# State-space stage: squares of x on 128 partitions, another place for the conditioning blocks and the tables of phases

## The reference, cut to what matters

```python
sh1, sc1, gt1, sh2, sc2, gt2 = adaln(c, w_mod[layer], b_mod[layer])       # c @ w_mod + b_mod, split in six
csh1, csc1, cgt1, csh2, csc2, cgt2 = adaln(c_ctx, w_mod[layer], b_mod[layer])
h_lat = modulate(rmsnorm(x_lat, norm_mix_pre[layer]), sh1[:, None], sc1[:, None])
h_ctx = modulate(rmsnorm(x_ctx, norm_mix_pre[layer]), csh1, csc1)
y_ctx, y_lat = s5_mixer(h_ctx, h_lat, s5_a_re[j], s5_a_im[j], ...)         # 128 groups of 16 columns, 64 complex states
```

## Time and profile before

| what | value |
|---|---|
| runs | 3567.32 us, the median of 3 (3565.69 to 3569.23) |
| profiled execution | 3563.7 us, 3.6 us under that median |
| its span, first to last instruction | 3561.5 us |
| granted clock of TensorE, mean | 0.954 of full speed |
| busy over the span | PE 92%, DVE 60%, ACT 39%, GpSimd 13% |
| chain that ended last, by engine | PE 82%, DVE 6%, GpSimd 5%, DMA 2% |

### The profile page before, as it was taken

One profiled execution on the slowest core, in us unless ns is written; L12 is line 12 of the kernel. 1 busy time (PEld: TensorE's weight loads), 2 busy tenths in 40 slices (PEclk: granted clock), 3 DMA queues, 4 the chain that ended last, 5 costly groups with the idle time before them and its releaser, 6 DMA issues.

```text
span 3561.5 us, 51912 instructions
## 1 busy us (share of the span) xinstructions
PE 3290.0 (92%) x21097; PEld 2763.7 (78%) x21097; DVE 2148.8 (60%) x1852; ACT 1386.6 (39%) x1390; POOL 480.1 (13%) x352
## 2 busy tenths in 40 slices
PE   5787889799999999886789999999989899999998
PEld 3445578688888888675678888888868788888887
DVE  7667755555555555699565555555654555555555
ACT  4446534433333333322234434433323344344332
POOL 2869900000000000096000000000000000000000
PEclk7789899899999999998799999999999999999999
DMA  9988865355555555344045555555524455555552
GB/s 304 299 279 255 262 219 188 94 188 182 185 189 188 188 188 188 107 141 148 33 156 168 186 189 188 185 190 184 184 92 141 140 183 186 188 188 188 189 183 89
DMA packets 351007, 643.12 MB, mean 181 GB/s; under 512 B 21599, under 2 KB 50359, under 8 KB 350519
## 3 DMA queue, kind: packets, MB, share of 16 engines
q1 hardware_dynamic: 309952, 561.68, 47.9%
q10 hardware_dynamic: 40951, 79.98, 6.6%
HBM read 637.54 MB, written 4.06 MB: 180 GB/s over the span
## 4 chain that ended last, share of the span: by engine, by line
PE 82%; DVE 6%; POOL 5%; issue 2%; DMA 2%; ACT 1%; DVEq 1%; SPq 0%; ACTq 0%; POOLq 0%
PE acc L436 49%; PE acc L437 25%; POOL cpow L1800 3%; DMA raw<-in_w_mod_dram 2%; POOL ptmp L1800 1%; DVE z L912 1%; DVE w_lo L758 1%; PE acc L1232 1%; PE acc L1249 1%; PE acc L516 1%; PE acc L528 1%; PE acc L459 1%; PE acc L1157 1%; PE acc L1216 1%; DVE hf L797 0%
## 5 line engine op out<-in xcount | busy, mean ns | idle before, releaser
L436 PE MATMUL acc<-xin,w_hi 128*128 128x512 f32 x5376 | 1914.6, 399 | 58.7 <-DVE xin L772 33.7
L758 DVE TENSOR_TENSOR w_lo<-raw,w_hi 128x2048 fp32r<-128x2048 f32 x488 | 1120.0, 2301 | 1082.0 <-ACT w_hi L612 1081.6
L437 PE MATMUL acc<-xin,w_lo 128*128 128x256 f32 x5376 | 1519.2, 283 | 0.0
L612 ACT ACTIVATE w_hi<-raw 128x2048 fp32r<-128x2048 f32 x488 | 934.2, 1917 | 1367.7 <-PE acc L437 1366.7
L436 PEld LDWEIGHTS acc<-xin,w_hi 128*128 128x128 f32 x5376 | 1016.8, 189 | 312.7 <-issue 36.5
L437 PEld LDWEIGHTS acc<-xin,w_lo 128*128 128x128 f32 x5376 | 1021.0, 190 | 0.0
L436 PE MATMUL acc<-hid,w_hi 128*128 128x512 f32 x2432 | 845.4, 392 | 0.0
L437 PE MATMUL acc<-hid,w_lo 128*128 128x256 f32 x2432 | 681.2, 280 | 0.0
L436 PEld LDWEIGHTS acc<-hid,w_hi 128*128 128x128 f32 x2432 | 455.1, 187 | 101.3
L437 PEld LDWEIGHTS acc<-hid,w_lo 128*128 128x128 f32 x2432 | 459.6, 189 | 0.0
L764 DVE TENSOR_REDUCE tmp<-acc 128x1024 f32<-128x2048 f32 x116 | 264.9, 2284 | 19.9 <-PE acc L437 19.9
(11 more groups left out here) (239 smaller groups left out, 2057.8 us busy)
## 6 DMA issues: line engine op xcount, KB each, us to landing
raw<-in_ffn_w_gate_dram SPq DMA_DIRECT2D x88, 1024.0 KB, 5.0
raw<-in_ffn_w_up_dram SPq DMA_DIRECT2D x88, 1024.0 KB, 5.0
raw<-in_ffn_w_down_dram SPq DMA_DIRECT2D x88, 1024.0 KB, 5.0
raw<-in_w_mod_dram ACTq DMA_DIRECT2D x76, 1024.0 KB, 9.0
raw<-in_w_mlp_in_dram SPq DMA_DIRECT2D x64, 1024.0 KB, 5.4
raw<-in_w_mlp_out_dram SPq DMA_DIRECT2D x64, 1024.0 KB, 5.0
raw<-in_s_w_glu_dram SPq DMA_DIRECT2D x32, 1024.0 KB, 5.4
raw<-in_ab_w_in_dram SPq DMA_DIRECT2D x32, 1024.0 KB, 5.3
```

What stands on the lines that cost most here:

```text
L436: pe.matmul(bank, w_hi[:, slot, w], operand[:, kt, :], start=(kt == 0), stop=False)
L437: ins = pe.matmul(bank[:, 0:TOK], w_lo[:, slot, w], operand[:, kt, 0:TOK], start=False, stop=(kt == UK * units - 1))
L612: act.activation(w_hi[:, slot, :], raw[:, slot, :, :].rearrange("p k n -> p (k n)"), ACT.Copy).then_inc(hi_ready, 1)
L758: dve.tensor_tensor(w_lo[:, slot, :], raw[:, slot, :, :].rearrange("p k n -> p (k n)"), w_hi[:, slot, :].bitcast(F32), SUB).then_inc(lo_re ...
```

## The change

- `xs` has 128 partitions. A partition holds four tokens of 2048 columns: partitions 0 to 63 take ctx, 64 to 127 take x. There are two transfers, of 64 partitions and 2 MB each, and both are issued ahead of block 0. Four squares of 128 partitions take the place of eight of 64. The sums (`ss_x`, 128 by 4) are turned into 64 by 8 by two small matmuls with `sel_g`, which PE does ahead of `ada_rows(0)`, behind waits for the squares and for `angle_ready`.
- On DVE the scaling of the sums comes ahead of `powers_of_b(0)`, and the reciprocal ahead of `powers` of `ab` 2 and 3. ACT takes the root ahead of `copy_adarow(0, 1)`.
- Blocks 0 and 1 alone are consumed ahead of the rounds. The other 22 are placed by `BLOCKS_OF`: one block in rounds 0, 1, 2, 4, 6, 8, 10, 12, 14 and 15, two in rounds 3, 5, 7, 9, 11 and 13. The MOD blocks are spread over rounds 0 to 5. The SP queue loads block 2 after x of tile 1; all later blocks are on ACT's queue as before.
- `mod_columns(1)` to `(3)` move from after the first `ada_rows` of rounds 0, 3 and 5 to between `states` and `outputs` of rounds 2, 4 and 6, and PE waits for `mod_raw` after `outputs`.

```diff
-        xs = Region(xin_at, xin_at + 32 * KB)("xs", [64, L // 2, D])
+        xs = Region(xin_at, xin_at + 32 * KB)("xs", [P, L // 2, D])
...
+        xwide = [v.rearrange("(c f j) d -> (c f) j d", f=2, j=L // 2) for v in (ctx2, x2)]
...
-        MOD = [(0, 1), (2, 3), (6, 8), (10, 12)]
-        ADA = [4, 5, 7, 9, 11] + list(range(13, 24))
...
+        BLOCKS_OF = [[("mod", 1, 0)], [("mod", 1, 1)], [("mod", 2, 0)], [("mod", 2, 1), ("ada", 0)], [("mod", 3, 0)],
+                     [("mod", 3, 1), ("ada", 1)], [("ada", 2)], [("ada", 3), ("ada", 4)], [("ada", 5)], [("ada", 6), ("ada", 7)],
+                     [("ada", 8)], [("ada", 9), ("ada", 10)], [("ada", 11)], [("ada", 12), ("ada", 13)], [("ada", 14)], [("ada", 15)]]
+        FIRST_BLOCK = [2 + sum(len(v) for v in BLOCKS_OF[:r]) for r in range(KT + 1)]
...
-                    sp.dma_start(xs[s * NCH:(s + 1) * NCH, :, :], xch[s][:, 4 * half:4 * half + 4, :]).then_inc(xs_in, 16)
+                    sp.dma_start(xs[s * 64:(s + 1) * 64, :, :], xwide[s]).then_inc(xs_in, 16)
...
-            load_xs(0)
+            load_xs()
             ada_units(sp, 0)
             load_c(0)
             load_x(0)
-            sp.wait_ge(xs_sq, 4)
-            load_xs(1)
             ada_units(sp, 1)
-            ada_units(sp, 2)
             sp.wait_ge(c_sel, 1)
             load_c(1)
-            ada_units(sp, 3)
             sp.wait_ge(xt_scaled, 1)
             load_x(1)
+            ada_units(sp, 2)
             sp.wait_ge(c_sel, 2)
             load_c(2)
-            ada_units(sp, 4)
...
-            mod_rows(0, 0)
-            mod_rows(0, 1)
+            pe.wait_ge(xs_sq, 4)
+            pe.wait_ge(angle_ready, 1)
+            for f in range(2):
+                ins = pe.matmul(ps[2][0:64, 4 * f:4 * f + 4], sel_g[:, f * 64:(f + 1) * 64], ss_x[:, :], start=True, stop=True)
+            ins.then_inc(ss_tr, 1)
+            ada_rows(0)
+            ada_rows(1)
...
-            mod_rows(1, 0)
...
-            mod_rows(1, 1)
...
+                    m, n_blocks = FIRST_BLOCK[k + 1], len(BLOCKS_OF[k + 1])
+                if k in (1, 3, 5):
+                    mod_columns((k + 1) // 2)
                 if k >= 0:
                     outputs(k, k % 2)
+                if k in (1, 3, 5):
+                    pe.wait_ge(mod_raw, (k + 3) // 2)
                 if k + 1 < KT:
...
-                if 0 <= k < 4:
-                    mod_rows(2 + k // 2, k % 2)
+                if k + 1 < KT and n_blocks == 2:
+                    ada_rows(m + 1)
...
-                if 0 <= k < 4:
-                    ada_units(act, ADA[k + 1] + 2)
...
+                if k + 1 < KT and len(BLOCKS_OF[k + 1]) == 2:
+                    ada_units(act, FIRST_BLOCK[k + 1] + 2)
...
+            dve.wait_ge(ss_tr, 1)
+            dve.tensor_scalar(rstd_x[:, :], ps[2][0:64, 0:L], 1.0 / D, EPS, MUL, ADD).then_inc(ss_ready, 1)
             powers_of_b(c0, 0)
-            dve.wait_ge(xs_sq, 8)
-            dve.tensor_scalar(rstd_x[:, :], rstd_x[:, :], 1.0 / D, EPS, MUL, ADD).then_inc(ss_ready, 1)
-            powers([ab[:, 2], ab[:, 3]], uu, L)
             dve.wait_ge(rstd_root, 1)
             dve.reciprocal(rstd_x[:, :], rstd_x[:, :]).then_inc(rstd_ready, 1)
+            powers([ab[:, 2], ab[:, 3]], uu, L)
             modulation(cm, 0)
```

More of the change, by code:

```diff
@@ L107, in two_layer_kernel @@
         rstd_x = whole("rstd_x", [64, L])
+        ss_x = whole("ss_x", [P, L // 2])
         work_at = whole.at
@@ L1060, in _, with load_xs @@
                 sp.dma_start(braw[:, ri, :, :], b_view[ri]).then_inc(b_in, 16)
-            def load_xs(half):
+            def load_xs():
                 for s in range(2):
-                    sp.dma_start(xs[s * NCH:(s + 1) * NCH, :, :], xch[s][:, 4 * half:4 * half + 4, :]).then_inc(xs_in, 16)
+                    sp.dma_start(xs[s * 64:(s + 1) * 64, :, :], xwide[s]).then_inc(xs_in, 16)
             def load_c(n):
@@ L1150, in select_c, with ada_rows @@
                 ins.then_inc(c_sel, 1)
-            def ada_rows(m, window, units=range(UK)):
+            def ada_rows(m, units=range(UK)):
+                window = BLOCK_WINDOW[m]
                 for kk in units:
@@ L1159, in ada_rows @@
                     ins.then_inc(ada_unit, 1)
-            def mod_rows(b, v):
-                ada_rows(MOD[b][v], 47 - (16 + 4 * b + 2 * v))
             def mod_columns(b):
@@ L1289, in _ @@
                     states(k + 1, (k + 1) % 2)
+                    m, n_blocks = FIRST_BLOCK[k + 1], len(BLOCKS_OF[k + 1])
+                if k in (1, 3, 5):
+                    mod_columns((k + 1) // 2)
                 if k >= 0:
                     outputs(k, k % 2)
+                if k in (1, 3, 5):
+                    pe.wait_ge(mod_raw, (k + 3) // 2)
                 if k + 1 < KT:
-                    if k in (-1, 2, 4):
-                        pe.wait_ge(ada_sb, {-1: 2, 2: 3, 4: 4}[k])
-                    ada_rows(ADA[k + 1], 15 - (k + 1), (0, 1))
-                if k in (-1, 2, 4):
-                    mod_columns({-1: 1, 2: 2, 4: 3}[k])
+                    ada_rows(m, (0, 1))
                 if k + 2 < KT:
@@ L1308, in _ @@
                 if k + 1 < KT:
-                    ada_rows(ADA[k + 1], 15 - (k + 1), (2, 3))
+                    ada_rows(m, (2, 3))
                 if k + 2 < KT:
                     transpose_e(k + 2, 1)
-                if 0 <= k < 4:
-                    mod_rows(2 + k // 2, k % 2)
+                if k + 1 < KT and n_blocks == 2:
+                    ada_rows(m + 1)
                 if k == KT - 2:
@@ L1356, in copy_adarow, with square_x @@
                 act.activation(adarow[:, :], ps[0][:, :], ACT.Copy).then_inc(ada_sb, 1)
-            def square_x(half):
-                act.wait_ge(xs_in, 32 * (half + 1))
-                for j in range(4):
-                    act.activation(xs[:, j, :], xs[:, j, :], ACT.Square, accum_out=rstd_x[:, 4 * half + j:4 * half + j + 1]).then_inc(xs_sq, 1)
+            def square_x():
+                act.wait_ge(xs_in, 32)
+                for j in range(L // 2):
+                    act.activation(xs[:, j, :], xs[:, j, :], ACT.Square, accum_out=ss_x[:, j:j + 1]).then_inc(xs_sq, 1)
             def block_diagonal_b(n):
@@ L1433, in _ @@
             copy_b(1)
-            square_x(0)
+            square_x()
             copy_b(2)
@@ L1444, in _ @@
             copy_lam_powers(0)
-            square_x(1)
-            copy_adarow(0, MOD[0][1])
+            act.wait_ge(ss_ready, 1)
+            act.activation(rstd_x[:, :], rstd_x[:, :], ACT.Sqrt).then_inc(rstd_root, 1)
+            copy_adarow(0, 1)
+            act.wait_ge(c_sel, 1)
             copy_modulation(0)
             copy_c(0, 0)
-            act.wait_ge(ss_ready, 1)
-            act.activation(rstd_x[:, :], rstd_x[:, :], ACT.Sqrt).then_inc(rstd_root, 1)
             act.wait_ge(rstd_ready, 1)
@@ L1468, in _ @@
                         copy_r8(k + 1)
+                    if k in (1, 3, 5):
+                        copy_modulation((k + 1) // 2)
                     gelu(k)
```

25 lines of the change are left out of this document (11 added, 14 removed).

## The result

The change makes the kernel slower by more than was forecast: 3612.12 us, median of 4 runs (3608.08 to 3614.09), against 3566.51 (3562.45 to 3569.23, 4 runs), ratio 1.0135, 95% interval 1.012 to 1.015. That is + 45.6 us, where 3588 was forecast with a range up to 3599. The profiled execution took 3614.09 us with a span of 3612.3; the profiled one before took 3563.7 with 3561.5, so the two traces differ by 50.8 us.

A forecast was written before the change was run, and what follows sets the result against it. Bound taken: a chain of waits over GpSimd and PE in one-block rounds, over the second block's late issue and transfer in two-block rounds. + 21.9 + 3.2 - 4.4 = + 20.7 us gave 3588, range 3570 to 3599.

The forecast's parts named there:

- The bound and the direction: Two-block rounds bound by the late issue plus transfer of their second block; kernel slower by 20.7 us, chance of slower 0.80.
- Part 1: Conditioning blocks respread, two-block rounds from 3 to 6 between lag 2 and lag 15: + 21.9 us, plus 3.2 for `mod_columns`.
- the hole: DMA engines nearly idle ahead of a two-block round's second block, 6 to 12 us in; claimed to stay where it is.
- The two-block round: Rounds 3, 5, 7, 9, 11 and 13: 29.2 us each, taken from round 2 before; bounds 23.9 and 31.2.
- The fourth rival: Two-block rounds like round 4 before, 31.2 us each, 12.0 us more than forecast: 3600; chance 0.08.
- The one-block rounds and `mod_columns`: Seven one-block rounds at 20.9 us each; `mod_columns` ahead of `outputs` in rounds 2, 4 and 6 adds 3.2 us.
- The prologue: Ahead of the rounds: `tables_ready` at 83.2, 4.4 us earlier, with lag 2 following at the same distance, at 134.9.
- The slow rate: Loads of x into 64 partitions run at the 197 GB/s of 32 partitions: 4 MB land at 32.4.
- the third rival: Loads of x ahead of the rounds at full rate, 387 GB/s: 7.0 us better than forecast, 3581; chance 0.15.
- Rivals 1 and 2: Two-block rounds: 1, 23.9 us each, 3556, chance 0.10; 2, 25.4 to 27 us, 3565 to 3575, chance 0.12.

The follow-up runs named there:

- e4_spread_only: The kernel before with only the new placement of the conditioning blocks, and `mod_columns` moved with it: 3602.84 us, ratio 1.0108.
- e2_noshift: The changed kernel with `ss_x` put at the end of the stage's own tiles, so later tiles keep their old place: 3593.69 us, ratio 1.0083.
- e5_wide: e2_noshift with each transfer of x into all 128 partitions and the sums regrouped by eight small matmuls: 3582.59 us, ratio 1.0048.
- e7_early: e2_noshift; in two-block rounds the first block is consumed whole behind `outputs` and all of the second issued there: 3574.83 us, ratio 1.003.
- e10_early_all: e7_early with its early issue in every round from 1 on: 3591.29 us, ratio 1.0082.
- e1_pad32: The kernel before with an unused tile of 128 by 4 ahead of the work tiles, moving them 32 bytes: 3578.03 us, ratio 1.004.

## Why the prediction was wrong, step by step

**The bound and the direction held.** Part 1 carries the loss (e4_spread_only), the long rounds end in waits of PE for `raw`, and the hole 6 to 12 us into them is there. It is by the steps of the sum that the time went astray: + 20.7 was forecast, + 50.8 came in the profiled execution, + 45.6 in the medians.

**The two-block round was mis-sized: 29.2 forecast, 31.8 measured, + 15.5 us over six rounds.** This is the step that failed first. The reason given for taking round 2 was that "its first block had landed by the time of the hole, as it will have behind a one-block round". It had not landed as early: the hole of round 5 had a share of 0.57 instead of 0.33. Round 2 before didn't follow a one-block round of 20 us either; it followed round 1, which GpSimd stretches to 31.7. The landings in the trace show what that changes. Before, the last two units of the first block were issued 5.9 and 2.9 us ahead of lag 2, and the last landed 7.6 us into the round. In the new round 5 they were issued 2.5 and 2.0 us ahead of the lag, two transfers of `xc` followed 1.2 and 1.8 us into the round (21 us in, before), and the last unit landed at 9.5. The store of `rw` landed at 10.2 instead of 8.0, `tw` could go out only then, and its last piece landed at 22.9 instead of 14.7, beside the second block. That the queue held a load when the round opened is not the difference: the first 5.7 us move 385 GB/s in round 2 before and 366 in the new round 5.

Over the six rounds the last unit is consumed 16.8 us later in sum than at round 2's 27.3. 8.7 of these are a later issue, nearly all in rounds 3 and 7 (15.4 and 16.8 us in, where round 2 had 12.0), and 8.1 a longer way from the issue to the last unit (16.4 to 17.7 us in rounds 5, 9, 11 and 13, where round 2 had 15.3). What the pauses of PE in rounds 3 and 7 cost is shown in part only. Round 7 lasts 33.5 and 34.7 us where it has the pause (the changed kernel, e2_noshift) and 29.5 and 30.6 where it has none (e4_spread_only, e5_wide). Round 3 lasts 30.8 with it in e4_spread_only and 32.1 without it in e5_wide. The split is read from the traces. Two things were tested: the issue of the second block sets the round (e7_early), and with the units ahead of the lag issued early too, the long rounds go from 28.3 to 27.0 us on the mean (e10_early_all), so what is carried over the lag is worth no more than some 1.2 us in each there. The fourth rival's 31.2 was the right size, at a chance of 0.08.

**The one-block rounds and `mod_columns` were over-sized: - 4.9 us.** 146.3 and 3.2 were forecast, 144.6 measured. The three rounds with `mod_columns` ahead of `outputs` last 23.1, 20.1 and 21.6, the other four 20.2, 20.0, 20.4 and 19.1, under the 20.9 taken; what one `mod_columns` costs was not measured by itself. In round 6 the chain of waits doesn't run over GpSimd, as the prediction had it, but from `mod_columns` over the modulation and some 8 us of `powers_of_b` on DVE.

**The prologue gave 1.5 us, not 4.4.** The slow rate was right (squares forecast at 32.4, seen at 33.6; the full rate, the third rival, didn't occur). Block 1's last unit was consumed until 60.0 instead of 58.1, `mraw` at 63.8 instead of 61.9, the first `phases` at 86.2 instead of 83.2. Block 1's first unit came at 50.2, 2.2 us later than forecast, and the delay ran through. The forecast let block 1 follow block 0 on the DMA engines. But a unit of it can only be issued when PE has consumed block 0's, and the change puts PE's first unit behind the squares, at 41.9; so block 1 was issued from 43.9 on (before: from 31.8), and until 47.4 the engines moved 251 GB/s. The DMA stretch of 58 to 66 at a share of 0.08 shows that there was nothing to load then: SP had block 2 behind the waits of its queue.

**A term was missing: + 16.2 us behind the stage.** The prediction held everything behind the stage constant, without a reason; this is the second step that failed. The 32 bytes alone cost 13.8 us (e1_pad32). The diff had the cause in it, a tile newly allocated ahead of the work tiles, and it was taken for bookkeeping. The sum of the four: 20.7 + 15.5 - 4.9 + 2.9 = 34.2, against 34.6 in the stage; with the missing term 50.8.

**The range** failed for two reasons: its upper end took in the bound of the long rounds only in part, and nothing in it stood for a change of place. With the 31.2 of rival 4 and the shift, 3600 + 14 = 3614 would have held the result; but that the two together come so near is seen only afterwards.

**Rivals 1 and 2** fell plainly. Rival 1 took the queues to be empty behind a one-block round, and the first 5.7 us of the new round 5 move 366 GB/s. No two-block round behind lag 2 came under 28.4 us in any kernel with the issue at its old place, and with the early issue the best was 26.1.

## What to carry to other kernels

A row taken as the price of a new round must come from a round with the same predecessor: ask which transfers stood in its queues when it opened and which small ones wait behind them, not only what it does itself. Spreading equal loads evenly gains nothing where the extra transfer is issued at a fixed late place; bringing its issue forward does (18 us here), and only where nobody then waits for the short round's own load. Any tile added ahead of the operands of the main matmuls is a change of its own: put it behind them, or time a few sizes of padding by themselves.
